# A convolution's 17-row remainders placed in four row groups, gate matmuls through three PSUM banks, and the sigmoid table's load moved

## The reference, cut to what matters

```python
n = rmsnorm(h, g_mix[l]);  proj = n @ w_in[l]
y_hy = hyena_branch(...)                       # below
y_rg = rglru_branch(...)                       # below
merged = sigmoid(gl_1) * y_hy + sigmoid(gl_2) * y_rg
h = h + merged @ w_out[l]
h = h + peer(rmsnorm(h, g_ffn[l]), ...)        # 128 gathered expert rows for each token

# hyena_filter: two sine layers on z (33 features x L positions), then a matmul and a decay
hdn = sin(freq[0] * (z @ w1 + b1));  hdn = sin(freq[1] * (hdn @ w2 + b2))
k = (hdn @ w3 + b3).reshape(L, 2, D_HY) * exp(-t * deltas)[:, None, :]
# fft_long_conv: U = rfft(u, n=2L), K = rfft(k_full), y = irfft(U * K)[:, :L] + u * skip

# rglru_direction: 4-tap causal convolution, then two gates for each of 8 heads of 128
gates = einsum('blhi,ghij->gblhj', xh, gate_w) + gate_b
r, i = sigmoid(gates[0]), sigmoid(gates[1])
a = exp(-8 r softplus(-lam));  h_t = a h_{t-1} + sqrt(1 - a^2) i x_t
```

## Time and profile before

| | us |
|---|---|
| median of 3 runs | 2143.38 |
| lowest and highest of them | 2132.02, 2146.47 |
| the profiled execution, its own time | 2133.56 |
| its span, first to last instruction | 2131.8 |
| TensorE busy | 1778.9 (83%) |
| VectorE busy | 807.5 (38%) |
| ScalarE busy | 423.8 (20%) |
| DMA moved | 761.06 MB, mean 357 GB/s |

### The profile page before, as it was taken

How to read it: one execution, slowest core, us unless ns; L and a number is a source line. 1 busy time by engine, 2 the same in 40 slices (tenths; PEclk the granted TensorE clock), 3 DMA queues, 4 the chain that set the end, 5 groups by cost and what they waited for, 6 DMA issues and landing times. The chain is left out here.

```text
span 2131.8 us, 23325 instructions
## 1 busy us (share of the span) xinstructions
PE 1778.9 (83%) x9360; PEld 902.4 (42%) x9360; DVE 807.5 (38%) x1930; ACT 423.8 (20%) x986; POOL 299.8 (14%) x284
## 2 busy tenths in 40 slices
PE   9999986876665566468999998888799999988887
PEld 7677772553331111124564433233277634323332
DVE  2756156776667777854230110010214401101002
ACT  2373123221112212222211000000124101000001
POOL 0000023443444444440000000000000000000000
PEclk9999998898888767889999999999999999999999
DMA  7236349999999999997779999999944799999997
GB/s 238 96 119 264 129 172 419 389 411 422 421 421 421 422 421 421 422 421 303 292 297 427 427 427 428 427 427 426 422 165 167 332 427 427 427 427 427 426 427 298
DMA packets 78687, 761.06 MB, mean 357 GB/s; under 512 B 8633, under 2 KB 9626, under 8 KB 17382
## 3 DMA queue, kind: packets, MB, share of 16 engines
q1 hardware_dynamic: 41046, 489.33, 55.0%
q0 software_dynamic: 37520, 270.11, 30.9%
HBM read 758.35 MB, written 1.05 MB: 356 GB/s over the span
## 5 line engine op out<-in xcount | busy, mean ns | idle before, releaser
L2550 PE MATMUL bank<-arena 128*64 128x512 f32 x3072 | 677.7, 595 | 72.0 <-DMA arena<-in_w_up 46.3
L1038 PE MATMUL bank<-arena 64*64 64x512 f32 x2032 | 321.6, 787 | 238.7 <-ACT arena L759 236.8
L2550 PEld LDWEIGHTS bank<-arena 128*64 128x64 f32 x3072 | 213.7, 137 | 523.3 <-issue 394.5
L554 POOL DMA_INDIRECT arena<-in_peer_uv,arena x256 | 288.1, 1125 | 655.7 <-PE bank L1038 307.6
L1373 DVE CUSTOM_DVE_ANT_0 arena<-arena 128x1024 f32<-128x1024 f32 x256 | 313.6, 1225 | 173.0 <-DMA arena<-in_peer_uv,arena 165.5
L1038 PEld LDWEIGHTS bank<-arena 64*64 64x64 f32 x2032 | 92.8, 176 | 448.5 <-ACT arena L759 264.6
L2662 DVE TENSOR_TENSOR arena<-arena,bank 128x512 f32<-128x512 f32 x32 | 22.0, 687 | 679.4 <-PE bank L2550 679.4
L809 PE MATMUL bank<-arena 128*128 128x272 f32 (+2 forms) x768 | 145.4, 349 | 0.5 <-ACT arena L586 0.3
L809 PEld LDWEIGHTS bank<-arena 128*128 128x128 f32 x768 | 126.2, 191 | 20.4 <-issue 3.2
L754 ACT ACTIVATE arena<-arena 128x4 f32<-128x4 f32 (+1 forms) x65 | 13.3, 205 | 465.6 <-DVE arena L1373 452.1
L1459 POOL DMA_DIRECT2D arena<-in_w_router x2 | 1.2, 577 | 577.7 <-POOLq L2440 542.0
(11 more groups left out here) (439 smaller groups left out, 1569.8 us busy)
## 6 DMA issues: line engine op xcount, KB each, us to landing
arena<-in_w_up SPq DMA_DIRECT2D x64, 2048.0 KB, 38.3
arena<-in_w_gate SPq DMA_DIRECT2D x64, 2048.0 KB, 39.2
arena<-in_w_down SPq DMA_DIRECT2D x64, 2048.0 KB, 40.7
arena<-in_w_in SPq DMA_DIRECT2D x14, 2048.0 KB, 8.1
arena<-in_w_out SPq DMA_DIRECT2D x2, 4096.0 KB, 18.0
arena<-in_wq SPq DMA_DIRECT2D x4, 2048.0 KB, 13.5
arena<-in_rg_out SPq DMA_DIRECT2D x1, 4096.0 KB, 12.4
arena<-in_peer_uv,arena POOLq DMA_INDIRECT x256
```

The costliest lines, as they stand in the source:

```text
L554: nc.gpsimd.indirect_dma_start(SLOT[slot_of[j]], None, d["peer_uv"], bass.IndirectOffsetOnAxis(IDX[:, u % 4, k:k + 1], 0)).then_inc(s_row[ ...
L1038: m = pe.matmul(bank[banks[t][half]][to:to + HALF, :], DIAG[lo:lo + HALF, k + j, :], row[lo:lo + HALF, D + half * 512:D + (half + 1) * 512 ...
L2550: x = pe.matmul(bank[b][j * C:(j + 1) * C, :], operand[:, c, j * C:(j + 1) * C], RING[s % AHEAD][:, c % (DC // 2), j, :], start=(c == 0), ...
```

## The change

Four edits, all in `front_stage` and its constants.

1. The rest of 17 positions is laid out four times, in partitions 0 to 16, 32 to 48, 64 to 80 and 96 to 112, with zeros to fill each group of 32. To get it there for the filter, the two sine layers run on `ZCOLS` = 383 columns instead of 272, the last `W3` products give 128 rows instead of 17, and the decay and `DFT_TAIL` come from DRAM with 128 rows instead of 17. For the input one copy on VectorE (`RESTS`, 128 x 512) spreads the rest before the transposes.
2. In `spectrum` the four `LOW_TAIL` products now come first, each in its own row group and into its own bank, and the four `LOW` products follow.
3. Gate n goes to bank 3, 2 or 4 by n % 3 and waits for the reader of gate n-3. The banks of the transposes move from 4, 5, 6 to 5, 6, 7. `gates(0)` no longer waits as a whole for `TOP_BANK`; gates 1 and 2 wait for the banks they take.
4. A Sigmoid on a single column (`WARM`) is issued before the filter's spectrum is read and once more behind `mult_root(0)`.

```diff
+ZCOLS = 2 * P - 1 + P
+    RESTS = cut(tmps, P, HT, P)
-    ARG = cut(spec, HY_FFN, L)
+    ARG = cut(spec, HY_FFN, ZCOLS)
...
+    GATE_BANKS, UT_BANKS = (3, 2, 4), (5, 6, 7)
-    LOW_TAIL = [DFT_TAIL[0:NTAIL, n * P:(n + 1) * P] for n in range(4)]
+    REST_ROWS = [slice(32 * n, 32 * n + NTAIL) for n in range(4)]
+    LOW_TAIL = [DFT_TAIL[REST_ROWS[n], n * P:(n + 1) * P] for n in range(4)]
...
-                pool.dma_start(DECAY[0:NTAIL, k, 2, :], d["decay"][k, 2 * P:, :]).then_inc(s_dft, 16)
+                pool.dma_start(DECAY[:, k, 2, :], d["decay"][k, 2 * P:, :]).then_inc(s_dft, 16)
-            pool.dma_start(DFT_TAIL[0:NTAIL, :], d["dft_tail"]).then_inc(s_dft, 16)
+            pool.dma_start(DFT_TAIL, d["dft_tail"]).then_inc(s_dft, 16)
...
             for n in range(6, 16):
                 tile_out(n)
+            a.activation(WARM, ONE, ACT.Sigmoid)
             act.wait_ge(s_kfm, 1)
...
-                a.activation(out, bank[2 + n % 2][:, 0:L], ACT.Sigmoid, bias=col("gbias", n)).then_inc(s_ga, 1)
+                a.activation(out, bank[GATE_BANKS[n % 3]][:, 0:L], ACT.Sigmoid, bias=col("gbias", n)).then_inc(s_ga, 1)
...
             mult_root(0)
+            a.activation(WARM, ONE, ACT.Sigmoid)
             for n in range(20, 24):
...
-                    pe.matmul(bank[7][0:HY_FFN, 0:L], W1, ZT, start=True, stop=True).then_inc(s_fmm, 1)
+                    pe.matmul(bank[7][0:HY_FFN, 0:ZCOLS], W1, ZT, start=True, stop=True).then_inc(s_fmm, 1)
...
                 for n in range(4):
-                    to = bank[SPEC_BANKS[n // 2][n % 2]][:, :]
-                    pe.matmul(to, LOW[n], folded[n], start=True, stop=False)
-                    pe.matmul(to, LOW_TAIL[n], rest[n], start=False, stop=True).then_inc(s_done, 1)
+                    pe.matmul(bank[SPEC_BANKS[n // 2][n % 2]][:, :], LOW_TAIL[n], rest[n][REST_ROWS[n], :], start=True, stop=False)
+                for n in range(4):
+                    pe.matmul(bank[SPEC_BANKS[n // 2][n % 2]][:, :], LOW[n], folded[n], start=False, stop=True).then_inc(s_done, 1)
...
-                    if n >= 2:
-                        te.wait_ge(s_ga, n - 1)
+                    if n >= 3:
+                        te.wait_ge(s_ga, n - 2)
+                    elif n:
+                        te.wait_ge(s_ksp, (KSP_TOP, KSP_TOP + 1)[n - 1])
                     if n < RH:
                         te.wait_ge(s_rgc, 8 * (n + 1))
-                    pe.matmul(bank[2 + n % 2][:, 0:L], GATEW[:, n, :], XC[:, dr * RH + h % RH, :],
+                    pe.matmul(bank[GATE_BANKS[n % 3]][:, 0:L], GATEW[:, n, :], XC[:, dr * RH + h % RH, :],
...
-            te.wait_ge(s_ksp, KSP_TOP)
             gates(0)
             project(4)
             project(5)
             gates(1)
-            te.wait_ge(s_u, HT + 3)
+            te.wait_ge(s_u, HT + 4)
             te.wait_ge(s_ksp, KSP_ALL)
             for c in range(3):
                 for t in range(HT):
-                    src = FOLDED[:, c, t, :] if c < 2 else HCV[:, t, P:P + NTAIL]
-                    m = pe.transpose(bank[4 + c][0:P if c < 2 else NTAIL, t * P:(t + 1) * P], src, ident)
+                    src = FOLDED[:, c, t, :] if c < 2 else RESTS[:, t, :]
+                    m = pe.transpose(bank[UT_BANKS[c]][:, t * P:(t + 1) * P], src, ident)
...
-                do(v.tensor_tensor(KFB[0:NTAIL, 0, k, :], bank[6 + k][0:NTAIL, :], DECAY[0:NTAIL, k, 2, :], ALU.mult))
+                do(v.tensor_tensor(KFB[:, 0, k, :], bank[6 + k][:, :], DECAY[:, k, 2, :], ALU.mult))
...
+            v.tensor_copy(RESTS.rearrange("p t (a b) -> p t a b", a=4),
+                          HCV[:, 0:HT, P:P + 32].unsqueeze(2).to_broadcast([P, HT, 4, 32])).then_inc(s_u, 1)
```

More of the change, by code:

```diff
@@ L293, in front_stage @@
     KSP = cut(spec, P, 2, 3, D_HY)
-    ARG = cut(spec, HY_FFN, L)
-    TURNS = cut(spec + L, HY_FFN, L)
+    ARG = cut(spec, HY_FFN, ZCOLS)
+    TURNS = cut(spec + ZCOLS, HY_FFN, ZCOLS)
     hc = spec + 2 * 3 * D_HY
@@ L300, in front_stage @@
     hids = hc + 3 * HT * L
-    ZT = cut(hids, HY_EMB, L)
-    HID = cut(hids, P, L)
-    assert hids + L <= nT
+    ZT = cut(hids, HY_EMB, ZCOLS)
+    HID = cut(hids, P, ZCOLS)
+    assert hids + ZCOLS <= nT
     GATEW = cut(gatew, P, 4 * RH, P)
@@ L846, in _ @@
             te.wait_ge(s_sin, 1)
-            pe.matmul(bank[6][0:HY_FFN, 0:L], W2, ARG, start=True, stop=True).then_inc(s_fmm, 1)
+            pe.matmul(bank[6][0:HY_FFN, 0:ZCOLS], W2, ARG, start=True, stop=True).then_inc(s_fmm, 1)
             tile(6)
@@ L851, in _ @@
             te.wait_ge(s_kpm, 1)
-            for c, cols in enumerate((slice(0, P), slice(P - 1, 2 * P - 1), slice(2 * P - 1, L))):
+            for c, cols in enumerate((slice(0, P), slice(P - 1, 2 * P - 1), slice(2 * P - 1, ZCOLS))):
                 if c == 2:
@@ L865, in spectrum @@
                 for n in range(4):
-                    m = pe.matmul(bank[TOP_BANK][TOP_ROWS[n], :], HIGH_TAIL[n], rest[n], start=False, stop=True)
+                    m = pe.matmul(bank[TOP_BANK][TOP_ROWS[n], :], HIGH_TAIL[n], rest[n][0:NTAIL, :], start=False, stop=True)
                 m.then_inc(s_done, 1)
                 for n in range(4):
-                    to = bank[SPEC_BANKS[n // 2][n % 2]][:, :]
-                    pe.matmul(to, LOW[n], folded[n], start=True, stop=False)
-                    pe.matmul(to, LOW_TAIL[n], rest[n], start=False, stop=True).then_inc(s_done, 1)
+                    pe.matmul(bank[SPEC_BANKS[n // 2][n % 2]][:, :], LOW_TAIL[n], rest[n][REST_ROWS[n], :], start=True, stop=False)
+                for n in range(4):
+                    pe.matmul(bank[SPEC_BANKS[n // 2][n % 2]][:, :], LOW[n], folded[n], start=False, stop=True).then_inc(s_done, 1)
             te.wait_ge(s_kpm, KPM_READY)
             te.wait_ge(s_dft, 16 * N_DFT)
-            spectrum([KPM[:, n % 2, FOLD[n], :] for n in range(4)], [KPM_TAIL[0:NTAIL, n % 2, :] for n in range(4)], s_kfm)
+            spectrum([KPM[:, n % 2, FOLD[n], :] for n in range(4)], [KPM_TAIL[:, n % 2, :] for n in range(4)], s_kfm)
             def gates(dr):
@@ L902, in _ @@
             te.wait_ge(s_ga, N_GATES)
-            spectrum([UTOK[:, FOLD[n], :] for n in range(4)], [UTOK[0:NTAIL, 2, :]] * 4, s_usm)
+            spectrum([UTOK[:, FOLD[n], :] for n in range(4)], [UTOK[:, 2, :]] * 4, s_usm)
             project(7)
@@ L1111, in _ @@
             ve.wait_ge(s_fmm, 1)
-            angle(bank[7][0:HY_FFN, 0:L], 0)
+            angle(bank[7][0:HY_FFN, 0:ZCOLS], 0)
             ve.wait_ge(s_el, 1)
@@ L1128, in _ @@
             ve.wait_ge(s_fmm, 2)
-            angle(bank[6][0:HY_FFN, 0:L], 2)
+            angle(bank[6][0:HY_FFN, 0:ZCOLS], 2)
             v.memset(HID[HY_FFN:HY_FFN + 1, :], 1.0).then_inc(s_kpm, 1)
@@ L1148, in _ @@
             for k in range(2):
-                do(v.tensor_tensor(KFB[0:NTAIL, 0, k, :], bank[6 + k][0:NTAIL, :], DECAY[0:NTAIL, k, 2, :], ALU.mult))
-            do(v.tensor_tensor(KPM_TAIL[0:NTAIL, 0, :], KFB[0:NTAIL, 0, 0, :], KFB[0:NTAIL, 0, 1, :], ALU.add))
-            v.tensor_tensor(KPM_TAIL[0:NTAIL, 1, :], KFB[0:NTAIL, 0, 0, :], KFB[0:NTAIL, 0, 1, :], ALU.subtract).then_inc(s_kpm, 1)
+                do(v.tensor_tensor(KFB[:, 0, k, :], bank[6 + k][:, :], DECAY[:, k, 2, :], ALU.mult))
+            do(v.tensor_tensor(KPM_TAIL[:, 0, :], KFB[:, 0, 0, :], KFB[:, 0, 1, :], ALU.add))
+            v.tensor_tensor(KPM_TAIL[:, 1, :], KFB[:, 0, 0, :], KFB[:, 0, 1, :], ALU.subtract).then_inc(s_kpm, 1)
             ve.wait_ge(s_kpm, KPM_READY)
@@ L1220, in _ @@
             ve.wait_ge(s_hyc, 9 * HT)
-            for c, n in enumerate((P, P, NTAIL)):
+            for c in range(3):
                 ve.wait_ge(s_utm, c + 1)
                 ve.wait_ge(s_rgc, 8 * RH)
-                v.tensor_copy(UTOK[0:n, c, :], bank[4 + c][0:n, :]).then_inc(s_ut, 1)
+                v.tensor_copy(UTOK[:, c, :], bank[UT_BANKS[c]][:, :]).then_inc(s_ut, 1)
             rg_input(1)
@@ L2788, in dft_constants @@
     dft_tail = np.concatenate([cos[:, even], sin[:, even], cos[:, odd], sin[:, odd],
-                               top(cos, 0), top(sin, 0), top(cos, 1), top(sin, 1)], 1)[rest].astype(f32)
+                               top(cos, 0), top(sin, 0), top(cos, 1), top(sin, 1)], 1)[rest]
     wcos, wsin = cos * w, sin * w
@@ L2804, in dft_constants, with in_quarters @@
     far = np.arange(L - 1, L - P, -1)
-    order = np.concatenate([np.arange(P), far, np.arange(P, P + NTAIL)])
+    order = np.concatenate([np.arange(P), far])
+    def in_quarters(a):
+        return np.tile(np.concatenate([a, np.zeros((32 - NTAIL, a.shape[1]))]), (4, 1)).astype(f32)
     lead = np.zeros((1, D_HY), f32)
-    decays = np.stack([np.concatenate([a[near], lead, a[far], a[rest]]) for a in (decay, back)])
-    return {"dft": dft, "dft_tail": dft_tail, "idft": idft, "zT": np.ascontiguousarray(zT[:, order]), "decay": decays}
+    decays = np.stack([np.concatenate([a[near], lead, a[far], in_quarters(a[rest])]) for a in (decay, back)])
```

(2 more changed lines are left out.)

## The result

| | before | after |
|---|---|---|
| median of 11 runs, us | 2132.02 | 2123.43 |
| lowest run, us | 2129.82 | 2119.77 |
| the profiled execution, us | 2133.56 | 2126.57 |
| its span, us | 2131.8 | 2124.9 |

The ratio after to before is 0.9948, with a 95% interval of 0.9932 to 0.9963: between 7.9 and 14.5 us faster, 11.1 in the middle. The medians differ by 8.6 us and the two profiled spans by 6.9. One of the eleven runs of the kernel after took 3452.64 us, for a reason that nothing here shows, and is left out of the ratio. The first three runs of the kernel before, which gave the 2143.38, were not typical: eleven give 2132.02.

What follows compares the result with a forecast made beforehand. TensorE's own list was taken to bound the front stage, gathered rows the time after. Gains of 0.7 + 4.2 + 3.8 = 8.7 us gave 2124.9 from the profiled execution, 2134.7 from the three-run median; stated 2133, range 2121 to 2143.

Steps and rivals of the forecast that it cites:

- The stated number: Time of the whole kernel after the change: 2133 us, with 8.7 us won in the sum.
- Second gates: Second gate group: early table load and third bank bring sixteen gates from 11.43 to 7.2 us, 4.2 us won.
- Input's spectrum: Input's spectrum on TensorE: packed row groups and new order bring it from 10.42 to 6.62 us, 3.8 us won.
- First gates: First gate group: VectorE's convolutions absorb the filter spectrum's gain, low clock follows; end at 105.9 against 106.63, 0.7 us won.
- Wider layers, more bytes, the RESTS copy: Filter layers, first transfers and VectorE's copy: 0.37 us on TensorE for wider W1 and W2; bytes and copy cost 0.
- Row groups without overlap: Both spectra: LOW_TAIL products run one by one, 3.6 us; total 6.1 us won, about 2136; chance 0.10.
- All nine gates at the low clock: First gates: all nine behind 100.2 run at 1.2 GHz, -1.6 instead of +0.7; about 2136; chance 0.12.
- The table doesn't stay: Both gate groups: another activation loads a table, the 1.4 us stall returns; total about 7 won, 2135; chance 0.07.
- The gain doesn't reach the end: Later stages: TensorE waits for scans or further on, leaving 2 to 6 us won; 2139; chance 0.06.
- Slower by a clock that stays low: Projections behind the first gates: clock stays low through project(4) and project(5), up to about +20, 2163; chance 0.03.

Runs made afterwards that it cites:

- The parts alone: Three kernels, each with only some of the edits: banks_only, table_only and packing_only; ratios to the kernel before 0.9965, 0.9984 and 0.9968.
- one_group: Kernel after with all four LOW_TAIL products in the first row group, same order and shapes; median 2126.12 us, ratio to the kernel before 0.9967.
- kept_busy: Kernel after with 12 small matmuls into a free bank before gate 6 and 12 before gate 7 of the first group; median 2121.90 us, ratio 0.9955.
- before_look4: Kernel before, unchanged, profiled again (third of four extra looks); 2134.26 us, span 2132.5.
- before_look5: Kernel before, unchanged, profiled again (last of four extra looks); 2125.52 us, span 2123.7.
- alternating_x6: Kernel after with the old alternating order in both spectra, its eight LOW and LOW_TAIL products issued six times over; one execution, 2286.18 us.
- packed_x6: Kernel after with LOW_TAIL in four row groups and then LOW, six times over in both spectra; one execution, clock 1.00 in both spectra.
- banks_only: Kernel before with the three gate banks and the moved transposes' banks alone; median 2125.36 us, ratio 0.9965, second gates 8.59 us.
- table_only: Kernel before with the two early Sigmoids alone; median 2129.10 us, ratio 0.9984, second gates 10.10 us.
- packing_only: Kernel after with two gate banks and without the early Sigmoids; median 2125.44 us, ratio to the kernel before 0.9968, second gates 11.43 us.
- by_head: Kernel after with the first group of gates issued by head, so two gates, not nine, follow VectorE's last head; median 2118.20 us, ratio 0.9935.
- before_look2: Kernel before, unchanged, profiled again (first of four extra looks); 2139.85 us, span 2138.1.

## Why the prediction was right or wrong

**The stated number.** This failed, at the last step of the sum: "against their median of 2143.38 it is 2134.7 ... so I state 2133". With 8.7 us won, 2133 presupposes a kernel before of 2141.7, and eleven runs of it give 2132.02, 9.7 lower; the median of three was 11 us too high. The rivals' times are reckoned from the same level and are too high by as much. The prediction gave no row for going from 2124.9 to 2133, only the spread of three runs. The sum itself, against the profiled execution (2133.56, typical as it turned out), gave 2124.9; the measured median is 2123.43. As a difference from 2132.02, the 2133 says "no gain", where the sum says 8.7 and the measurement 8.6 by the medians, 11.1 (7.9 to 14.5) by the ratio. The measured time lies in the range of 2121 to 2143, in its lower part. That the sum comes so near is in part luck: one of its terms was 1.0 us too large, below, and it left out something that varies by 9.9 us from execution to execution.

**Second gates.** 4.2 forecast, 4.09 measured. The parts alone bear out the round trip (10.10 with two banks) and the table's 1.3 to 1.4.

**Input's spectrum.** 3.8 forecast, 3.83 measured; the packed group 1.06 us against the 0.99 taken over from the column groups, and the LOW products behind it 3.54 against 3.65. The Trainium skill's figure of 3.07 times (TensorE: Matmul & The Clock Gate, Measured speedup vs the span model), by which I had estimated 1.37 us, would make the packed group slower than the 1.06 us of this trace; the measurement decides. That row tiles run side by side, which the figure rests on, one_group bears out.

**First gates.** The mechanism was right: VectorE's chain takes the gain, the waits bring the clock down (kept_busy). That a wait is followed by the low clock was read from one execution, though, and it isn't a rule: before_look4 and before_look5 have the same wait of 1.48 us and stay at 1.00. The size was off: I forecast an end at 105.9, 0.7 won, and it came at 106.92, 0.3 lost. Of this 1.0 us, gate 7 starts 0.35 later than the 100.2 forecast, and 0.7 is the low clock, which cost the nine gates 6.4 us instead of 5.7: at 0.895 and 0.448 us a gate that is about 5.2 of them at 0.50, where I had 3.8. Measured from the spectrum's start, A, the change wins 0.05 us; against a profile of the kernel before at 1.00, 22.19, it loses 0.84. With -0.3 + 4.1 + 3.8 = 7.6 the three terms account for the 7.7 us at the mixer's output product.

**Wider layers, more bytes, the RESTS copy.** Each of the two wider products takes 0.85 us instead of 0.67, together 0.36 us (0.37 forecast). The first line is the kernel before, the second the kernel after:

```profile
23.31 0.67 PE L842 MATMUL bank<-arena 33*64 33x272 f32 x2
23.58 0.85 PE L848 MATMUL bank<-arena 33*64 33x383 f32 x2
```

The spectrum starts 0.34 us later, but its start varies by 1.8 us between the profiles of the kernel before, so that agreement says little. No transfer ended a wait of TensorE before 300 us, and the RESTS copy held nothing up: the bytes and the copy cost nothing, as forecast.

**What the sum lacked.** The kernel before pays for the alternation a second time, by the clock, in some executions. Over its five profiles C is 167.7 on average; less 158.0, and less the 0.36 of the wider layers ahead of C, this is 9.3 us won; against the shortest C it is 6.8, against the longest 16.7. This spread is the kernel before's own. I had named "a granted clock" only behind waits. That five profiles of one kernel and one of the other carry the right average isn't shown; that the alternation lowers the clock and the packed order doesn't, alternating_x6 and packed_x6 show, with one execution each. The spreads of whole runs lean the same way: the kernels with the alternation in both spectra spread over 17.8 us (before, 31 runs), 16.7 (banks_only) and 14.4 (table_only), while after and packing_only spread over 6.8 and kept_busy over 5.5, ten runs each. They prove little: by_head, without the alternation, spreads over 10.8 in six runs.

**The rivals.** Row groups without overlap: refuted by one_group. All nine gates at the low clock: about five of them were, 6.4 us where nine at 0.50 would take 8.1 and none 4.0. The table doesn't stay: refuted, no load before a gate. The gain doesn't reach the end: 7.7 us at the mixer's output product, 6.9 in the span; the difference is within what the later part varies by. Slower by a clock that stays low: it didn't happen behind the waits (1.00 again from 104.5 on), though such a price exists, 17 us at 0.50 in banks_only and 13 in before_look2; but it is the kernels with the alternation that pay it.

## What to carry to other kernels

When a stage is shortened, look at the engine that has run beside it: here the first spectrum's 3.8 us came to nothing until three heads of VectorE's chain were moved into VectorE's own idle time; then, by the trace, nothing stood between the spectrum and the gates. Small products with few rows cost three times over: their own time, the change of shape, and in some executions the clock of the work behind them. Packed in row groups, four of them cost 1.06 us and one change of shape, and the clock stayed at 1.00 (packed_x6). And an estimate is to be anchored on the execution that it was read from, or on many runs, not on the median of three.

## What the runs showed that I had not expected

TensorE's clock falls to 0.50 with the engine busy without a gap: between 2.3 us (banks_only) and 10.6 us (alternating_x6) behind the start of alternating 17-row and 128-row products, 2 us into 17-row products alone, and not in 41 us of full ones or in 28 us of packed and full ones. It stayed low for 17 us in banks_only, through full-size projection work too. Where a wait is followed by the low clock, a slower stage ahead of the wait can end the stage sooner (one_group's first gates, 20.88 us against 23.03).
